# Attention on one core: both value parts in one stationary operand, and one channel summed on GpSimd

## The chip, the cores and the metric

The kernel runs on one core of one Trainium2 chip. A core has five engines that run beside each other: TensorE (PE: matmuls into PSUM), VectorE (DVE), ScalarE (ACT), GpSimd (POOL), and SyncE (SP), which here issues the DMA transfers. The metric is device time in microseconds of one execution, as the median of the runs.

## The reference

One step of a hybrid encoder layer for a prompt of 2048 rows and a sample of 32 rows with 2048 cached rows. A front stage normalises the rows and projects them. The change lies in the prompt's attention, eight heads of width 64:

```python
logits = einsum('bqhd,bkhd->bhqk', qblk, k) * scale
logits = logits + cq[..., None] - ck[:, :, None, :]     # running sums of log forget gates
logits = where(k_pos <= q_pos, logits, -inf)
probs = softmax(logits, axis=-1)
att = einsum('bhqk,bkhd->bqhd', probs, v)
...
y_b = att * silu(z_b)
```

Matrices are fp32, and the kernel splits each operand of a product into a high part that TensorE takes (fp32r) and the low rest, and adds three products: high by high, high by low, low by high.

## The kernel before, in words

**Stages.** The program is written out by hand for each engine, as one list of instructions with semaphore waits; nothing is scheduled by a planner. The front stage runs to about 1070 us of the trace, the prompt's attention (`prompt_attention`) from 1071.7 to about 1478 us, then come the sample's attention, the merge and the output norm.

**A head.** The eight heads run one after the other. A head has 40 steps: four query blocks q = 0 to 3 of 512 queries, and in block q the key blocks kb = 0 to 4q+3 of 128 keys. Steps 0 to 3 are q = 0, 4 to 11 are q = 1, 12 to 23 are q = 2, and 24 to 39 are q = 3. The last four key blocks of each q lie on the diagonal and are 512, 384, 256 and 128 columns wide; the other 24 steps of a head are 512 wide. In a step:

- TensorE makes the scores of the step three ahead (`scores`, L1668 and L1669, and a small mask matmul L1671 on the diagonal) into one of four PSUM banks, at most two row-maximum tiles for the next head (`unit`, L1701), and three value products for this step (`values`, L1685 to L1687) into one of two PSUM banks `o_bank`.
- ScalarE takes the exponential twice (`probs`, L1747 and L1748), once as the rounded high part `p_hi` and once whole.
- VectorE subtracts to get `p_lo` (`low`, L1778), reduces the row-maximum tiles (L1786, L1789; 40 in a head, in steps 0 to 29), copies a finished `o_bank` to SBUF (`take`, L1809) and, after step 9's work (`INVERT = 9`), takes the reciprocal of the last head's sums (`invert`, L1768).
- GpSimd scales, gates and splits the last head's rows (L1847, L1852, L1856), at steps set by `FINISH`.

`p_hi`, `p_lo` and the score banks are rings of four slots. The stationary operand of a value product has 64 value columns; the other 64 columns are ones in `v_hi` and zeros in `v_lo`, so that row 64 of `o_bank` is the softmax's sum.

**SyncE's list for a head h** (`sync`), in order: store the fourth sum of head h-1, load the sums as columns (L1587), store the reciprocals (L1591), load them as rows (L1595), load `zb` (L1624), the six loads of head h+1 (`load_main`, L1611 and L1613), three loads of head h+2 (`load_max`, L1605), further loads for the sample in heads 1 and 7, and then stores of sums and of the last head's rows. An issue waits for its turn in this one list. Each transfer of the six is 512 KB.

The functions that the change touches follow with the profile's line numbers.

## Time and profile before

| What | us |
|---|---|
| median of 3 runs | 1914.37 (1910.13 to 1914.48) |
| the profiled execution | 1912.48, of which span 1910.5 |
| prompt's attention in it | 1071.7 to about 1478 |
| a middle head in it (first value product to the next head's) | about 52 |

The span is the time from the first to the last instruction that the profiler saw. A group of rows below is a part of one view of that execution. A start is counted from the span's start. "idle before" is the time in which an engine waited, with what ended the wait.

### The profile page before, as it was taken

How to read it: one execution, taken by the hardware profiler on the slowest of the kernel's cores; microseconds unless marked ns; L12 is line 12 of the kernel's file. 1: busy time of each engine (PE TensorE's matmuls, PEld its weight loads, DVE VectorE, ACT ScalarE, POOL GpSimd, SP SyncE). 2: the span in 40 equal slices, each digit the busy share in tenths (PEclk: the TensorE clock that was granted, in tenths of full speed). 3: DMA queues.
4: the chain of work that ended last, by engine and by line, in shares of the span. 5: the costliest groups of instructions: out<-in, count | busy, mean ns of one | idle time of the engine just before them, and what ended most of it. 6: DMA issues, size and time to landing. Idle time of an engine off the chain costs nothing.

```text
span 1910.5 us, 28723 instructions
## 1 busy us (share of the span) xinstructions
PE 1862.7 (97%) x10604; PEld 1724.0 (90%) x10604; DVE 1295.1 (68%) x2255; ACT 854.3 (45%) x1594; POOL 185.9 (10%) x153
## 2 busy tenths in 40 slices
PE   7899999999999999999999999999999899999998
PEld 6899999999999999999999787788778799998885
DVE  8878787954545365444656588888896734457887
ACT  5545546634344443433323577777778600111100
POOL 1000000000000000000000202333333400000111
PEclk9999999999999999999999999999999999999999
DMA  6798897969889886879897816666654796765442
GB/s 225 242 329 287 314 327 278 319 233 321 269 289 315 286 297 219 298 236 326 265 303 236 211 28 121 127 134 134 134 106 142 235 377 218 246 183 160 142 144 74
DMA packets 272782, 435.99 MB, mean 228 GB/s; under 512 B 63252, under 2 KB 139188, under 8 KB 268508
## 3 DMA queue, kind: packets, MB, share of 16 engines
q1 hardware_dynamic: 266884, 425.64, 71.0%
q10 hardware_dynamic: 5760, 8.52, 1.2%
q8 instruction: 85, 1.39, 0.3%
q14 instruction: 53, 0.43, 0.1%
HBM read 285.18 MB, written 148.78 MB: 227 GB/s over the span
## 4 chain that ended last, share of the span: by engine, by line
PE 81%; DVE 7%; DMA 4%; SPq 2%; issue 2%; ACT 2%; POOL 1%; POOLq 0%; DVEq 0%; ACTq 0%
PE fr_b L639 4%; PE fr_c L639 4%; PE fr_b L640 4%; PE fr_b L641 4%; PE fr_c L640 4%; PE fr_c L641 4%; PE fr_a L640 4%; PE fr_a L639 4%; PE fr_a L641 4%; PE ln_b L2541 3%; PE ln_b L2543 3%; PE ln_b L2542 3%; PE at_o L1685 3%; PE at_m L1701 3%; PE at_s L1669 3%; PE at_s L1668 3%
## 5 line engine op out<-in xcount | busy, mean ns | idle before, releaser
L815 ACT ACTIVATE fr_wq<-fr_raw 128x512 fp32r<-128x512 f32 x288 | 178.3, 628 | 208.9 <-PE fr_d L641 137.9
L1778 DVE TENSOR_TENSOR at_p_lo<-at_s,at_p_hi 128x512 fp32r<-128x512 f32 (+1 forms) x320 | 191.9, 603 | 42.7 <-ACT at_s L1748 41.1
L1747 ACT ACTIVATE at_p_hi<-at_s 128x512 fp32r<-128x512 f32 (+1 forms) x320 | 169.8, 531 | 83.7 <-PE at_s L1669 49.1
L1105 DVE TENSOR_TENSOR fr_wq<-fr_raw,fr_wq 128x512 fp32r<-128x512 f32 x288 | 192.2, 683 | 11.4 <-ACT fr_wq L815 8.2
L639 PE MATMUL fr_b<-fr_xh,fr_wq 128*128 128x348 f32 x568 | 185.4, 326 | 7.8 <-DVE fr_wq L1105 4.0
L639 PE MATMUL fr_a<-fr_xh,fr_wq 128*128 128x348 f32 x568 | 183.9, 324 | 0.6 <-ACT fr_p L898 0.6
L639 PE MATMUL fr_c<-fr_xh,fr_wq 128*128 128x348 f32 x568 | 183.7, 323 | 0.4 <-DMA fr_wq<-w_mixed 0.4
L640 PE MATMUL fr_a<-fr_xl,fr_wq 128*128 128x348 f32 x568 | 183.4, 323 | 0.0
L641 PE MATMUL fr_b<-fr_xh,fr_wq 128*128 128x348 f32 x568 | 183.4, 323 | 0.0
L640 PE MATMUL fr_b<-fr_xl,fr_wq 128*128 128x348 f32 x568 | 183.2, 323 | 0.0
L641 PE MATMUL fr_a<-fr_xh,fr_wq 128*128 128x348 f32 x568 | 182.8, 322 | 0.0
L640 PE MATMUL fr_c<-fr_xl,fr_wq 128*128 128x348 f32 x568 | 182.4, 321 | 0.0
L641 PE MATMUL fr_c<-fr_xh,fr_wq 128*128 128x348 f32 x568 | 182.2, 321 | 0.0
L1748 ACT ACTIVATE at_s<-at_s 128x512 f32<-128x512 f32 (+1 forms) x320 | 168.7, 527 | 0.0
L1291 DVE TENSOR_TENSOR fr_res<-fr_c,fr_u 128x348 f32<-128x348 f32 x71 | 36.9, 520 | 175.8 <-PE fr_c L641 175.6
L1685 PE MATMUL at_o<-at_p_hi,at_main 128*128 128x512 f32 (+1 forms) x320 | 123.4, 386 | 0.5
L1786 DVE TENSOR_REDUCE at_piece_max<-at_m 128x1 f32<-128x512 f32 x168 | 114.3, 683 | 6.1 <-PE at_m L1701 5.9
L1669 PE MATMUL at_s<-at_qm,at_km 68*128 68x512 f32 (+1 forms) x320 | 117.8, 368 | 0.0
L1668 PE MATMUL at_s<-at_main 128*128 128x512 f32 (+1 forms) x320 | 117.6, 367 | 0.1
L975 ACT ACTIVATE fr_res<-fr_a 128x348 f32<-128x348 f32 x71 | 32.7, 461 | 189.7 <-PE fr_a L641 183.0
L1686 PE MATMUL at_o<-at_p_lo,at_main 128*128 128x512 f32 (+1 forms) x320 | 117.3, 367 | 0.0
L1687 PE MATMUL at_o<-at_p_hi,at_main 128*128 128x512 f32 (+1 forms) x320 | 117.1, 366 | 0.0
(390 smaller groups left out, 4681.3 us busy)
## 6 DMA issues: line engine op xcount, KB each, us to landing
fr_wq<-w_mixed SPq DMA_DIRECT2D x192, 512.0 KB, 5.5
fr_raw<-w_tiles SPq DMA_DIRECT2D x96, 512.0 KB, 5.2
w_mixed<-fr_wq SPq DMA_DIRECT2D x96, 512.0 KB, 4.6
mg_gates<-merge_gates SPq DMA_DIRECT2D x40, 416.0 KB, 4.8
fr_raw<-w_tiles SPq DMA_DIRECT2D x48, 256.0 KB, 5.3
merge_gates<-fr_res SPq DMA_DIRECT2D x32, 348.0 KB, 6.3
mixed<-mg_mixed ACTq DMA_DIRECT2D x40, 208.0 KB, 4.2
ln_h<-h_rows SPq DMA_DIRECT2D x16, 512.0 KB, 3.3
```

Of the source, the lines that this page charges most:

```text
L639: pe.matmul(to, wh[:, idx, k, :], xh[:, idx, k, :], start=first, stop=False, skip_group_check=skip)
L640: pe.matmul(to, wh[:, idx, k, :], xl[:, idx, k, :], start=False, stop=False, skip_group_check=skip)
L641: last = pe.matmul(to, wl[:, idx, k, :], xh[:, idx, k, :], start=False, stop=end, skip_group_check=skip)
L815: act.activation(wh[:, idx], operand(i, idx), ACT.Copy).then_inc(w_hi[idx], 1)
L1105: dve.tensor_tensor(wl[:, idx], operand(i, idx), wh[:, idx].bitcast(F32), ALU.subtract).then_inc(w_lo[idx], 1)
L1668: pe.matmul(bank[:, cols], ks[:, b, keys], qs[:, b, asked], start=True, stop=False)
L1669: last = pe.matmul(bank[:, cols], km[h % 3][:, keys], qm[h % 3][:, asked], start=False, stop=not diagonal)
L1685: pe.matmul(o, v_hi[:, b, kb, :], p_hi[:, r, cols], start=(kb == 0), stop=False)
L1686: pe.matmul(o, v_hi[:, b, kb, :], p_lo[:, r, cols], start=False, stop=False)
L1747: act.activation(p_hi[:, r, cols], s_bank[r][:, cols], ACT.Exp, scale=SCALE)
L1748: act.activation(s_bank[r][:, cols], s_bank[r][:, cols], ACT.Exp, scale=SCALE).then_inc(p_done, 1)
L1778: dve.tensor_tensor(p_lo[:, r, cols], s_bank[r][:, cols], p_hi[:, r, cols].bitcast(F32), ALU.subtract)\
```

## The change

A value product's stationary operand now holds both parts of the values: columns 0 to 63 the high part and 64 to 127 the low part (`v_both`). One product with `p_hi` and one with `p_lo` give high by high, low by high and both with `p_lo`, in rows 0 to 63 and 64 to 127 of `o_bank`. The first low channel (column 64) is overwritten with ones, so that row 64 is still the sum. What this channel would have given is made in another way: in most steps by a third product with `v_first`, which has that channel in column 0 and zeros elsewhere; in the steps for which `pooled` holds (odd kb off the diagonal: steps 5 and 7, 13, 15, 17, 19, and 25, 27, 29, 31, 33, 35) GpSimd multiplies `p_hi` with the channel and adds it up in `acc` (`first_channel`), and one more product for each of q = 1, 2, 3 brings `acc` into row 0 (`close`).

The two halves of `o_bank` are added: ScalarE copies the upper rows to `part`, one of eight buffers (`copy_part`), and `take` becomes a multiply-and-add of `part` and `o_bank` (`lanes` is one, and zero for row 64). Sums, reciprocals and their transfers go by the block q in place of once for a head, and the tables `INVERT` to `TAKE_AT` say at which step of which head (0 this one, 1 the one before) each is done. SyncE's list has another order. In the front stage the first head's low values are loaded right behind its high ones. In the diff below a line of "..." stands for lines left out.

```diff
             def load_lead_v(x, of):
-                sp.dma_start(v0[x][:, :, 0:HD].bitcast(F32), of[0:SEQ, 0:HD].rearrange("(b p) c -> p b c", p=P))\
+                at = slice(x * HD, (x + 1) * HD)
+                sp.dma_start(v0[0][:, :, at].bitcast(F32), of[0:SEQ, 0:HD].rearrange("(b p) c -> p b c", p=P))\
                   .then_inc(lead.v_in, 16)
...
         ks, qs = main[:, :, 0], main[:, :, 1]
-        v_hi, v_lo = (main[:, :, 2 + x].rearrange("p a (b c) -> p a b c", c=P) for x in range(2))
+        v_both, v_first = (main[:, :, 2 + x].rearrange("p a (b c) -> p a b c", c=P) for x in range(2))
+        first_row = sb("first_row", [P, P], 29184, F32R)
+        acc = sb("acc", [P, QW], 29312, F32R)
+        lanes = sb("lanes", [P, 1], 29824)
+        part = sb("part", [P, 2 * NQ, QW], 34880)
...
-        INVERT = 9
-        FINISH = {20 + 4 * q + x + x // 2: (q, x) for x in range(3) for q in range(NQ)}
-        FINISH_LOW = {st + 5: q for st, (q, x) in FINISH.items() if x == 0}
+        INVERT = {15: (0, 0), 23: (0, 1), 33: (0, 2), 12: (1, 3)}
+        SCALE_AT = {22: (0, 0), 37: (0, 1), 0: (1, 2), 20: (1, 3)}
+        GATE_AT = {23: (0, 0), 38: (0, 1), 1: (1, 2), 21: (1, 3)}
+        UPPER_AT = {26: (0, 0), 0: (1, 1), 4: (1, 2), 23: (1, 3)}
+        LOWER_AT = {36: (0, 0), 2: (1, 1), 8: (1, 2), 24: (1, 3)}
+        V_AT = 10
+        PART_AT = {(e + 5) % NS: (0 if e + 5 < NS else 1, q) for q, e in enumerate(ends)}
+        TAKE_AT = {(e + 4) % NS: (0 if e + 4 < NS else 1, q) for q, e in enumerate(ends)}
         TURN = 32
+
+        def pooled(st):
+            q, kb = steps[st]
+            return kb < 4 * q and kb % 2 == 1
+
...
+        def added_through(h, q):
+            return pooled_through(h, ends[q]) - 3 * h - q
+
+        def at_step(plan, h, st):
+            back, q = plan.get(st, (0, None))
+            h -= back
+            return (h, q) if q is not None and h >= 0 else None
...
+        def sums_load(sp, h, q):
+            sp.wait_ge(sum_out, 16 * (NQ * h + q) + 16)
+            sp.dma_start(sums[:, 4 * q:4 * q + 4], s["sums"][h:h + 1, q * QW:(q + 1) * QW].rearrange("a (p b) -> (a p) b", p=P))\
+              .then_inc(sums_in[q], 16)
...
+        def rcp_load(sp, h, q):
+            sp.wait_ge(rcp_out, 16 * (NQ * h + q) + 16)
+            if h:
+                sp.wait_ge(y_scaled, NQ * (h - 1) + q + 1)
+            sp.dma_start(rcp_all[:, q * QW:(q + 1) * QW], s["rcps"][h:h + 1, q * QW:(q + 1) * QW].broadcast_to([HD, QW]))\
+              .then_inc(rcp_in[q], 16)
...
             for h in range(H):
                 if h == 0:
                     sp.dma_start(mask[:, :], causal).then_inc(const_in, 16)
-                if h:
-                    sum_store(sp, h - 1, 3)
-                    sums_load(sp, h - 1)
-                    rcp_store(sp, h - 1)
-                    rcp_load(sp, h - 1)
+                if h > 1:
+                    sp.wait_ge(y_gated, NQ * (h - 1))
                 sp.dma_start(zb[:, h % 2], s["zb"][h * HD:(h + 1) * HD, 0:SEQ]).then_inc(zb_in[h % 2], 16)
                 if h + 1 < H:
                     if h:
-                        sp.wait_ge(pv_done, NS * h + RING)
+                        sp.wait_ge(closed, 3 * h)
                     load_main(h + 1)
                 if h + 2 < H:
                     if h == 0:
...
                 if h == H - 1:
                     sam.key_loads(sp)
+                if h:
+                    sum_store(sp, h - 1, 3)
+                    y_store(sp, h - 1, 1)
+                    sums_load(sp, h - 1, 3)
                 sum_store(sp, h, 0)
+                if h:
+                    y_store(sp, h - 1, 2)
+                sums_load(sp, h, 0)
+                if h:
+                    rcp_store(sp, h - 1, 3)
+                    rcp_load(sp, h - 1, 3)
+                rcp_store(sp, h, 0)
                 sum_store(sp, h, 1)
+                rcp_load(sp, h, 0)
+                sums_load(sp, h, 1)
+                rcp_store(sp, h, 1)
                 if h:
-                    y_store(sp, h - 1, 0)
...
                     max_rows(sp, h + 1)
-                if h:
-                    y_store(sp, h - 1, 2)
-                    y_store(sp, h - 1, 3)
+                rcp_load(sp, h, 2)
+                if h < H - 1:
+                    y_store(sp, h, 0)
...
                 cols = slice(d * P, QW)
                 if h == 0 and st == 0:
                     pe.wait_ge(lead.v_in, 32)
+                if st == 0:
+                    pe.wait_ge(v_ready, 2 * h + 2)
                 if kb == 0:
                     pe.wait_ge(o_read, NQ * h + q + 1)
                 pe.wait_ge(lo_done, NS * h + st + 1 + RING)
                 r = st % RING
                 o = o_bank[q % 2][:, cols]
-                pe.matmul(o, v_hi[:, b, kb, :], p_hi[:, r, cols], start=(kb == 0), stop=False)
-                pe.matmul(o, v_hi[:, b, kb, :], p_lo[:, r, cols], start=False, stop=False)
-                pe.matmul(o, v_lo[:, b, kb, :], p_hi[:, r, cols], start=False, stop=(kb == 4 * q + 3))\
-                  .then_inc(pv_done, 1)
+                pe.matmul(o, v_both[:, b, kb, :], p_hi[:, r, cols], start=(kb == 0), stop=False)
+                last = pe.matmul(o, v_both[:, b, kb, :], p_lo[:, r, cols], start=False, stop=False)
+                if not pooled(st):
+                    last = pe.matmul(o, v_first[:, b, kb, :], p_hi[:, r, cols], start=False, stop=(q == 0 and kb == 3))
+                last.then_inc(pv_done, 1)
+
+            def close(h, q):
+                if h == 0 and q == 1:
+                    pe.wait_ge(first_row_set, 2)
+                pe.wait_ge(acc_done, added_through(h, q))
+                pe.matmul(o_bank[q % 2][:, :], first_row[:, :], acc[:, :], start=False, stop=True).then_inc(closed, 1)
 
...
                     values(h, b, st)
+                    if h and st == 0:
+                        close(h - 1, NQ - 1)
+                    if st - 1 in ends[1:-1]:
+                        close(h, ends.index(st - 1))
...
+                before = (h, st - RING) if st >= RING else (h - 1, st - RING + NS)
+                if before[0] >= 0 and pooled(before[1]):
+                    act.wait_ge(acc_scaled, pooled_through(*before))
                 act.activation(p_hi[:, r, cols], s_bank[r][:, cols], ACT.Exp, scale=SCALE)
                 act.activation(s_bank[r][:, cols], s_bank[r][:, cols], ACT.Exp, scale=SCALE).then_inc(p_done, 1)
+
+            def copy_part(h, q):
+                n = NQ * h + q
...
+                    act.wait_ge(o_read, n - 2 * NQ + 3)
...
             def take(h, b, q):
-                dve.wait_ge(pv_done, NS * h + ends[q] + 1 + RING)
+                dve.wait_ge(part_done, NQ * h + q + 1)
                 if h > 1:
                     dve.wait_ge(yl_done, NQ * (h - 1))
-                dve.tensor_copy(y[:, b, q * QW:(q + 1) * QW], o_bank[q % 2][0:HD + 1, :]).then_inc(o_read, 1)
+                o = o_bank[q % 2]
+                dve.scalar_tensor_tensor(out=y[0:HD, b, q * QW:(q + 1) * QW], in0=part[HD:2 * HD, (NQ * h + q) % (2 * NQ), :], scalar=lanes[HD:2 * HD, :],
+                                         in1=o[0:HD, :], op0=ALU.mult, op1=ALU.add).then_inc(o_read, 1)
...
+            def free_first_channel(h):
+                b = h % 2
+                if h:
+                    pool.wait_ge(main_in[b], used(h, 2, 96))
+                else:
+                    pool.wait_ge(lead.v_in, 32)
+                pool.tensor_copy(v_first[:, b, :, 0:1], v_both[:, b, :, HD:HD + 1].bitcast(F32)).then_inc(v_ready, 1)
+                pool.wait_ge(v_ready, 2 * h + 1)
+                pool.memset(v_both[:, b, :, HD:HD + 1].bitcast(F32), 1.0).then_inc(v_ready, 1)
...
-            for h in range(1, H):
+            def first_channel(h, st):
+                q, kb = steps[st]
+                r, n = st % RING, pooled_through(h, st)
+                own = v_first[:, h % 2, kb, 0:1].bitcast(F32)
+                pool.wait_ge(p_done, NS * h + st + 1)
+                if kb == 1:
+                    if n > 1:
+                        pool.wait_ge(closed, 3 * h + q - 1)
+                    pool.tensor_scalar(acc[:, :], p_hi[:, r, :].bitcast(F32), own, None, ALU.mult).then_inc(acc_scaled, 1)
+                else:
+                    added = n - 3 * h - q
+                    if added > 1:
+                        pool.wait_ge(acc_done, added - 1)
+                    pool.tensor_scalar(term[:, :], p_hi[:, r, :].bitcast(F32), own, None, ALU.mult).then_inc(acc_scaled, 1)
+                    pool.wait_ge(acc_scaled, n)
+                    pool.tensor_tensor(acc[:, :], acc[:, :].bitcast(F32), term[:, :], ALU.add).then_inc(acc_done, 1)
+
+            for h in range(H):
                 for st in range(NS):
-                    if st in FINISH_LOW:
-                        lower(pool, h - 1, 1 - h % 2, FINISH_LOW[st])
-                    if st in FINISH and FINISH[st][1] < 2:
-                        (scale, gate)[FINISH[st][1]](pool, h - 1, 1 - h % 2, FINISH[st][0])
+                    if h + 1 < H and st == V_AT:
+                        free_first_channel(h + 1)
```

SyncE's list at a middle head before, from the loads of the next head on: `sums` is the store of a block's sums, `at_sums` the load of sums that the reciprocal reads, `yb_hi` and `yb_lo` the stores of finished rows.

```order
L1591 DMA rcps<-at_rcp 128x16
L1595 DMA at_rcp_all<-rcps 64x2048
L1624 DMA at_zb<-silu_zb 64x2048
L1611 DMA at_main<-k_hi 64x2048
L1611 DMA at_main<-q_lo 64x2048
L1611 DMA at_main<-k_lo 64x2048
L1611 DMA at_main<-q_hi 64x2048
L1613 DMA at_main<-v_hi 128x16x64
L1613 DMA at_main<-v_lo 128x16x64
L1605 DMA at_km_50<-k_hi 64x2048
L1605 DMA at_qm_52<-q_hi 64x2048
L1605 DMA at_km_50<-forget_rows 2x2048
```

The same place of the change, from the second of the six loads on:

```order
L1636 DMA at_main<-q_lo 64x2048
L1636 DMA at_main<-k_lo 64x2048
L1636 DMA at_main<-q_hi 64x2048
L1638 DMA at_main<-v_hi 128x16x64
L1638 DMA at_main<-v_lo 128x16x64
L1630 DMA at_km_50<-k_hi 64x2048
L1630 DMA at_qm_52<-q_hi 64x2048
L1630 DMA at_km_50<-forget_rows 2x2048
L1602 DMA sums<-at_part 1x512
L1597 DMA yb_hi<-at_y_hi 64x512
L1597 DMA yb_lo<-at_y_lo 64x512
L1607 DMA at_sums<-sums 128x4
```

Before, the reciprocals of the last head were stored and loaded ahead of the nine loads; now the store of that head's fourth block of sums, two row stores and the load `at_sums` for the fourth reciprocal stand behind them.

VectorE's list before, around the reciprocal (`RECIPROCAL`), in a middle head; a 128x256 subtraction is that of step 10, so this is the end of step 9's work:

```order
L1778 TENSOR_TENSOR at_p_lo<-at_s,at_p_hi 128x256
L1786 TENSOR_REDUCE at_piece_max<-at_m 128x1
L1768 RECIPROCAL at_rcp<-at_sums 128x16
L1778 TENSOR_TENSOR at_p_lo<-at_s,at_p_hi 128x128
L1786 TENSOR_REDUCE at_piece_max<-at_m 128x1
L1778 TENSOR_TENSOR at_p_lo<-at_s,at_p_hi 128x512
```

The change's reciprocals of the last head's fourth block and of this head's first block:

```order
L1855 TENSOR_REDUCE at_piece_max<-at_m 128x1
L1837 RECIPROCAL at_rcp<-at_sums 128x4
L1847 TENSOR_TENSOR at_p_lo<-at_s,at_p_hi 128x512
L1858 ISA at_m,at_piece_max<-at_m,at_wide_mask 128x256
L1858 ISA at_piece_max 128x1
L1847 TENSOR_TENSOR at_p_lo<-at_s,at_p_hi 128x512
L1855 TENSOR_REDUCE at_piece_max<-at_m 128x1 x2
L1847 TENSOR_TENSOR at_p_lo<-at_s,at_p_hi 128x512
L1858 ISA at_m,at_piece_max<-at_m,at_wide_mask 128x384
L1858 ISA at_piece_max 128x1
L1879 SCALAR_TENSOR_TENSOR at_y<-at_part,at_lanes,at_o 64x512
L1837 RECIPROCAL at_rcp<-at_sums 128x4
```

The reciprocal that needs the last block of the head before has moved from the end of step 9's work to the end of step 12's, behind three more subtractions and four more reductions.

## Rows read from the trace of the kernel before

**Rows 1.** The page, busy time, share of the span and instructions of engines.

```profile
PE 1862.7 (97%) x10604; PEld 1724.0 (90%) x10604; DVE 1295.1 (68%) x2255; ACT 854.3 (45%) x1594; POOL 185.9 (10%) x153
```

**Rows 2.** Windows: start:end, us, busy of PE, PEld, DVE, ACT, POOL, clock, DMA share, GB/s.

```profile
1276.00:1328.00 52.00, 51.86 (x259) 41.62 (x259) 46.50 (x104) 39.77 (x86) 15.32 (x13) 1.00 0.60 123
...
1435.00:1478.00 43.00, 43.00 (x226) 35.59 (x225) 27.03 (x46) 37.64 (x84) 15.24 (x12) 1.00 0.51 151
```

**Rows 3.** Windows inside the middle head, about steps 0-11, 12-30, 31-39.

```profile
1281.00:1296.20 15.20, 15.15 (x80) 12.46 (x79) 14.38 (x40) 10.83 (x25) 0.00 (x0) 1.00 0.02 2
1296.20:1322.00 25.80, 25.80 (x121) 20.53 (x120) 25.19 (x53) 20.04 (x40) 12.62 (x10) 1.00 1.04 204
1322.00:1332.90 10.90, 10.81 (x62) 8.56 (x60) 7.08 (x16) 8.82 (x22) 2.63 (x3) 1.00 0.37 102
```

**Rows 4.** Timeline of TensorE, same head: start us, duration us.

```profile
1280.97 0.44 PE L1685 MATMUL at_o<-at_p_hi,at_main 128*128 128x512 f32 x1
...
1287.33 0.40 PE L1685 MATMUL at_o<-at_p_hi,at_main 128*128 128x512 f32 x1
...
1287.80 0.39 PE L1687 MATMUL at_o<-at_p_hi,at_main 128*128 128x512 f32 x1
```

**Rows 5.** Timeline of VectorE, same head, from the reciprocal to step 12's last reduction.

```profile
1293.95 0.24 DVE L1768 RECIPROCAL at_rcp<-at_sums 128x16 f32<-128x16 f32 x1
...
1297.18 0.68 DVE L1786 TENSOR_REDUCE at_piece_max<-at_m 128x1 f32<-128x512 f32 x1
```

**Rows 6.** Timeline of SyncE's DMA issues, same head: start us, duration us of an issue.

```profile
1295.65 0.48 SPq L1595 DMA_DIRECT2D at_rcp_all<-rcps  x1
1296.17 0.60 SPq L1624 DMA_DIRECT2D at_zb<-silu_zb  x1
1296.82 0.60 SPq L1611 DMA_DIRECT2D at_main<-k_hi  x1
...
1300.18 12.62 SPq L1613 DMA_DIRECT2D at_main<-v_lo  x1
1317.50 0.54 SPq L1582 DMA_DIRECT2D sums<-at_y  x2
```

**Rows 7.** DMA issues of that head: KB each, median us from issue to landing.

```profile
at_main<-v_lo SPq DMA_DIRECT2D x1, 512.0 KB, 20.4
```

**Rows 8.** The same, of 1317.3 to 1319.2 us alone.

```profile
yb_hi<-at_y_hi SPq DMA_DIRECT2D x1, 128.0 KB, 5.4
```

**Rows 9.** The tile yb_hi: landing of all its stores.

```profile
DMA to landing us min/median/max: 2.2/2.4/12.1
```

**Rows 10.** The tile at_sums: landing of all its loads.

```profile
DMA to landing us min/median/max: 1.5/1.6/4.3
```

**Rows 11.** SyncE's waits, six heads: us in total, times, longest.

```profile
SPq L1587 <- DMA sums<-at_y: 5.4, 6, 0.9
```

**Rows 12.** SyncE's issues in head 1: the sample's early loads, first issue and the issue behind.

```profile
1160.14 2.04 SPq L1969 DMA_DIRECT2D sa_q_hi<-q_hi  x2
...
1167.92 0.35 SPq L1582 DMA_DIRECT2D sums<-at_y  x1
```

**Rows 13.** SyncE's issues in head 7: first key load and the issue behind them.

```profile
1448.02 4.85 SPq L1981 DMA_DIRECT2D sa_k_rows<-cache_k  x4
...
1457.27 0.56 SPq L1582 DMA_DIRECT2D sums<-at_y  x2
```

**Rows 14.** Windows around the start of attention: columns as in rows 3.

```profile
1064.00:1067.40 3.40, 0.00 (x0) 0.01 (x1) 0.52 (x1) 0.49 (x1) 0.02 (x1) 1.00 1.19 238
...
1071.60:1075.00 3.40, 3.40 (x10) 2.92 (x11) 1.25 (x6) 1.04 (x4) 2.61 (x4) 0.50 1.11 273
```

**Rows 15.** Groups by form, GpSimd: count, busy us, mean ns, idle before.

```profile
L1847 POOL TENSOR_TENSOR at_y<-at_y,at_rcp_all 64x512 f32<-64x512 f32 x32 | 42.0, 1317 | 213.7 <-DMA at_rcp_all<-rcps 213.7
...
L1865 POOL MEMSET at_main<- 128x1024 f32 x1 | 1.0, 957 | 0.1
```

**Rows 16.** Groups by form, VectorE: the copy of o_bank.

```profile
L1809 DVE COPY at_y<-at_o 65x512 f32<-65x512 f32 x32 | 21.8, 681 | 1.9 <-PE at_o L1687 1.9
```

More of the change, by code:

```diff
@@ L1760, in scalar, with invert @@
                         copy_rows(h + 1)
[L1761 to L1765 removed]
+                    if at_step(PART_AT, h, st):
+                        copy_part(*at_step(PART_AT, h, st))
+                    job = at_step(UPPER_AT, h, st)
+                    if job and job[0] < H - 1:
+                        upper(act, job[0], job[0] % 2, job[1])
+            copy_part(H - 1, NQ - 1)
+        def invert(dve, h, q):
+            dve.wait_ge(sums_in[q], 16 * h + 16)
             if h:
[L1767 to L1768 removed]
+                dve.wait_ge(rcp_out, 16 * (NQ * (h - 1) + q) + 16)
+            dve.reciprocal(rcp[:, 4 * q:4 * q + 4], sums[:, 4 * q:4 * q + 4]).then_inc(rcp_done, 1)
         st_.invert = invert
@@ L1869, in gpsimd @@
             sam.clear_queries(pool)
-            for h in range(1, H):
-                for st in range(NS):
-                    if st in FINISH_LOW:
-                        lower(pool, h - 1, 1 - h % 2, FINISH_LOW[st])
-                    if st in FINISH and FINISH[st][1] < 2:
-                        (scale, gate)[FINISH[st][1]](pool, h - 1, 1 - h % 2, FINISH[st][0])
+            def first_channel(h, st):
[7 more added lines that the diff above has]
+                    pool.tensor_scalar(acc[:, :], p_hi[:, r, :].bitcast(F32), own, None, ALU.mult).then_inc(acc_scaled, 1)
+                else:
+                    added = n - 3 * h - q
[5 more added lines that the diff above has]
+            for h in range(H):
+                for st in range(NS):
+                    if h + 1 < H and st == V_AT:
+                        free_first_channel(h + 1)
+                    if pooled(st):
+                        first_channel(h, st)
+                    for plan, what in ((LOWER_AT, lower), (SCALE_AT, scale), (GATE_AT, gate)):
+                        job = at_step(plan, h, st)
+                        if job and job[0] < H - 1:
+                            what(pool, job[0], job[0] % 2, job[1])
         st_.sync, st_.tensor, st_.scalar, st_.vector, st_.gpsimd = sync, tensor, scalar, vector, gpsimd
```

103 lines of the change are left out of this document (52 added, 51 removed).

## The prediction

> **What bounds the kernel now.** I read the page first: TensorE is busy for 97% of the span, VectorE for 68% and GpSimd for 10% [rows 1]. That speaks for taking products from TensorE and giving work to GpSimd. But the 97% is a mean over stages, so I next read windows of the stage that is changed. In a middle head of 52.0 us TensorE is busy 51.86 and VectorE 46.50; in the last head, which has no row-maximum tiles to reduce, VectorE has only 27.03 of 43.0 [rows 2]. Cut into three, the middle head shows two bounds: VectorE is busy 14.38 of 15.2 us in the first third and 25.19 of 25.8 in the second, and only 7.08 of 10.9 in the last, where ScalarE has 8.82 [rows 3]. So a product taken from TensorE shows in full only where VectorE has room, about steps 31 to 39. Last I read who feeds VectorE: its reciprocal waits for a load that SyncE issues from one list, so SyncE's issues and their landings are part of the path as soon as that load is late.
>
> **What is saved.** Two products of 512 columns start 0.47 us after each other (1287.33 to 1287.80), so one costs 0.235 us [rows 4]. The change takes 12 of them from a head and adds 3 closing ones: 9 x 8 x 0.235 = 16.9 us of TensorE's time in all. Of this, steps 5 and 7 lie in the first third and seven of the twelve in the second. There VectorE, whose work doesn't shrink, has 0.8 and 0.6 us left, so I count 0.5 us for both. In the last third three products fall away, 0.7 us. VectorE gains three small reciprocals a head; the present one takes 0.24 us and the next instruction followed it within that time [rows 5], so 0.5 us more. That leaves 0.7 us for each of seven heads, and 2 us for the last, where only ScalarE, at 37.64 of 43.0, is near: together 7 us. The bounds are 16.9 (VectorE never in the way) and 2 (only the last head). The multiply-and-add that takes the place of the copy is not in the trace; the copy takes 681 ns [rows 16], and I take the same, with the reading of a second operand from SBUF as the doubt that the lower bound covers. ScalarE's four copies a head lie in its free 12 us [rows 2].
>
> **GpSimd.** A head gets 12 multiplications and 9 additions of 128x512. The nearest rows are a two-input operation of 64x512 at 1317 ns and a memset of 128x1024 at 957 ns, so 0.48 for 512 columns [rows 15]: an addition is taken at 1.32, a multiplication lies between 0.48 and 1.32. With 12 scale, gate and split operations of 1.32 the head's sum is 33 to 44 us of 52, so it has room on average and costs nothing where nothing else is late; if it were the bound, ScalarE would wait for it, since a slot of `p_hi` is refilled four steps later. The Trainium skill, GPSIMD Engine Reference, section 3.1, gives 769 ns for a one-input loop over 512 elements: by that a multiplication would be 0.77 us and the sum would stay as it is.
>
> **What becomes late.** This is the large term. `at_sums` of the last head's fourth block now stands in SyncE's list behind the nine loads for later heads, and VectorE waits for it at the end of step 12's work. I set both on one clock, from the head's first value product at 1280.97 [rows 4].
>
> VectorE's side: step 12's last reduction starts at 1297.18, and the one-after-another pace is 0.6 us (subtraction and reduction overlap a little), so VectorE asks at about 1297.8, which is +16.8 [rows 5].
>
> SyncE's side: the loads may start when the head before is closed, after the first products, at about +1.2 (three products and a closing one, 0.94 us, and the semaphore). In the trace 20.7 us pass between the issue of the first of the six loads and that of the sums behind the nine (1296.82 to 1317.50), above all because the issue of `v_lo` is held for 12.62 us [rows 6]. There, two transfers of 512 KB, `rcp_all` and `zb`, had been issued within 1.2 us ahead of them. The window moves 204 GB/s [rows 3], so one such transfer takes 2.6 us, and without both the distance would be 15.5. In the change `zb` and a row store still go ahead but some 2 us earlier; I take 17. The sums are then issued at +18.2. A store that was issued at that place landed after 5.4 us [rows 8], where such stores take 2.4 in the median and 12.1 at most [rows 9]; so it lay 3 us behind what was in the queue. The sums alone land within about 1.1 (0.22 for the issue and a wait of at most 0.9 [rows 11]); behind the loads 4.2, at +22.4. `at_sums` then needs 0.35 for its issue and 1.6 us to land [rows 10]: +24.4. VectorE waits 24.4 - 16.8 = 7.6 us. TensorE has about 1.2 us of work in hand meanwhile (five products, 5 x 0.235), so 6.4 us are lost. At the low end (distance 15.5, landing 1.1, load 1.5) the sums are there at +19.7 and 1.7 are lost; at the high end (20.7, 5.4, 4.3) at +32, and 14 are lost. Behind the waiting reciprocal stand all of VectorE's subtractions, so every engine waits, and VectorE has no room in the second third to win it back.
>
> By head: heads 2 to 5 lose 4 x 6.4 = 25.6. In head 1 the sample's early loads stand in the same list, 7.8 us of issues (1160.14 to 1167.92) [rows 12], while the queue drains: issue at +26, landing 2, load 2, so +30, less 16.8 and 1.2: 12. In head 6 three of the nine loads are missing, 4.7 us of issues (1312.80 to 1317.50) [rows 6]; the queue is then longer, 5 us to land: +20.4, 2.4 lost. In head 7 the key loads take 9.25 us of issues [rows 13]; 1 + 9.25 + 5 + 2 = +17.2 against VectorE's asking at about +13, since its steps take five products, 1.2 us: 3 lost. Head 0 asks only for its own first block, after step 15, and its loads start ahead of the head: 0.5, at most 3. Sum 43.5 us (low end 16, of which head 1 has 9.5; high end about 90).
>
> **The clock.** Before attention TensorE is idle for the 3.40 us from 1064.0; a few us later its granted clock is 0.50, which is 1.2 GHz, from 1071.6 to 1075.0, with 10 products in 3.4 us [rows 14]. Stalls of 6 us in heads 1 to 5 may do the same. At half the clock at most half of such a stretch's work is lost, 1.7 us; I take 1.6 for each of five heads, 8 us (0 to 22, if all seven stalls cost two such stretches).
>
> **The sum.** 43.5 + 8 - 7 = +44.5 on the profiled execution's 1912.48: 1957. That execution lies 0.1% below the median of the runs, which changes nothing here.
>
> **The rivals.** (A) Faster: the sums come in time. This needs them by +16.8 and so 7.6 us earlier than I have them; then only the saving is left, 1912.5 - 7 = 1905 (1896 if it shows in full). For it speaks that the queue is clear when the loads start earlier; against it, that even the low end is late by 2.9 us. The Trainium skill, DMA: Bandwidth & Descriptors, section Bandwidth, has 341 GB/s for a load of 1 MB; by that the nine loads would be through in about three fifths of the time, and the sums just in time. The trace has 204 GB/s in that very window, and I go by the trace. (B) No change: the sums come in time, but GpSimd's wait for the next head's values at step 10 (`V_AT`) takes the place. `v_lo` landed 23.8 us after the first load's issue (1300.18 + 20.4 - 1296.82) [rows 6, 7]; less 3.7 as above, that is +21.3. After two small operations and a multiplication, at +23, ScalarE may refill step 17's slot, about 2 us after it would; six heads lose 2 each, 1912.5 + 12 - 7 = 1918. In my forecast this wait lies inside VectorE's longer one. (C) Slower still: GpSimd at its upper price and blocked from about +9 to +21 needs 44 + 12 = 56 us of a head that lasts 52 + 7; it decides only from 59 us on, and would then add 2 to 4 us a head, some 20: 1977.
>
> **How the numbers follow.** My forecast has 0.76, A 0.10, B 0.07, C 0.07. The time is the forecast's, 1957. The range runs from 1912, where the low end of the waits meets the full saving (1912.5 + 16 + 0 - 16.9), to 2000, past C and most of the way to the high end (1912.5 + 90 + 22 - 2 = 2022, which needs every bound at once). It leaves out A and the last tail, some 15 in 100. A change under 0.3% (5.7 us) can't be told from none here: faster 0.10 (A), same 0.07 (B), slower 0.83.
>
> **What would show it.** Right: VectorE's reciprocal waits for `at_sums` seven times, 2 to 13 us each, longest in head 1; SyncE's issue of `v_lo` still takes over 10 us; heads 1 to 5 last 57 to 64 us; after some stalls the granted clock falls. Wrong: `at_sums` lands before VectorE asks, heads under 52 us; or the longest wait in a head is ScalarE's for GpSimd; or subtractions, 0.68 us now, get longer beside GpSimd's new work.

## The result and the profile after

The changed kernel takes 1998.98 us (1997.66 to 2003.53, 4 runs) against 1912.43 (1910.13 to 1914.48, 4 runs) of the kernel before: a ratio of 1.0463, with an interval of 1.0446 to 1.048. The forecast was +44.5 us; it is +86.5. The profiled execution has a span of 2001.7 us. Its page, engines and the granted clock in 40 slices, beside [rows 1]:

```profile
PE 1895.4 (95%) x10532; PEld 1736.4 (87%) x10532; DVE 1307.8 (65%) x2281; ACT 872.6 (44%) x1626; POOL 428.1 (21%) x337
PEclk8999999999999999999998988898989999999999
```

The clock row of the kernel before:

```profile
PEclk9999999999999999999999999999999999999999
```

TensorE is busy longer with 72 matmuls fewer, and from the 22nd to the 30th slice, which is attention, the clock row has 8s. All of the loss lies there. From the first to the last value product attention took 405.4 us before and takes 499.2; from then to the end it is 433.4 and 433.5. The table cuts each head by the starts of its first value products (us, summed over eight heads; the granted clock's record gives the last column):

| | steps 0-11 | 12-23 | 24-30 | 31-39 | sum | at half clock |
|---|---|---|---|---|---|---|
| before | 123.8 | 128.6 | 77.3 | 75.7 | 405.4 | 3.3 |
| after | 174.0 | 170.9 | 80.3 | 73.9 | 499.2 | 104.3 |

A middle head (head 4) lasts 65.4 us instead of 51.9. Windows of its steps 0 to 11, 12 to 30 and 31 to 39, as [rows 3]:

```profile
1325.70:1347.30 21.60, 17.67 (x83) 13.97 (x81) 15.44 (x40) 14.64 (x33) 11.94 (x10) 0.92 1.00 198
1347.30:1381.80 34.50, 28.43 (x119) 21.87 (x118) 26.43 (x57) 21.39 (x42) 24.96 (x20) 0.90 0.28 57
1381.80:1391.10 9.30, 9.08 (x53) 6.92 (x53) 6.04 (x12) 6.04 (x16) 8.71 (x7) 1.00 0.05 16
```

No engine is busy throughout in the first two any more: everyone waits. In the last third, where VectorE had room, 0.4 us is gained (the windows here and in [rows 3] are cut at slightly different places; by the starts of the value products, steps 31 to 39 of head 4 took 9.8 and take 9.4). Three waits of the view of waits, over all of attention (us in total, times, longest), show on whom:

```profile
POOL at_main L1941 <- DMA at_main<-v_lo: 47.7, 7, 9.4
ACT at_y_hi L1782 <- POOL at_y L1925: 36.5, 14, 3.7
DVE at_rcp L1837 <- DMA at_sums<-sums: 28.2, 7, 7.3
```

The third is the wait that was forecast: seven times, six of them behind step 12 and one in head 0, for its own first block. The second was not: ScalarE, in order, waits at the split of the last head's rows for GpSimd's gate. The chain of waits that ends with the sums that VectorE needs in head 4, in order of time:

```profile
1331.25 10.54 SPq L1638
...
1341.83 3.27 SPq L1630
...
1345.78 0.46 SPq L1630
1346.24 0.04 issue
1346.29 6.57 DMA sums<-at_part
1352.86 0.02 issue
1352.88 1.58 DMA at_sums<-sums
1354.46 0.02 issue
1354.48 0.18 DVE at_rcp L1837
...
1356.48 0.43 PE at_o L1724
```

The issue of `v_lo` is held for 10.54 us, the sums' 2 KB need 6.57 us behind the loads, and VectorE starts its reciprocal at +28.8 from the head's first value product (1325.7). In the last row it is 0.43 us from the start of a value product of 512 columns to the next; at the full clock it was 0.235 [rows 4]. Windows around that wait show why (the clock is the third number from the end):

```profile
1344.60:1348.00 3.40, 3.40 (x20) 2.78 (x19) 3.31 (x9) 2.88 (x6) 0.00 (x0) 1.00 1.11 222
1348.00:1351.40 3.40, 2.13 (x10) 1.44 (x8) 0.47 (x1) 2.45 (x5) 2.42 (x4) 1.00 0.92 201
1351.40:1354.80 3.40, 0.00 (x0) 0.00 (x0) 0.32 (x2) 0.67 (x2) 3.15 (x3) 0.92 0.18 53
1354.80:1358.20 3.40, 2.51 (x6) 2.03 (x7) 3.17 (x7) 0.00 (x0) 1.97 (x2) 0.50 0.35 72
1358.20:1361.60 3.40, 3.40 (x10) 2.74 (x10) 2.56 (x6) 2.01 (x4) 0.00 (x0) 0.58 0.15 39
1361.60:1365.00 3.40, 3.40 (x19) 2.53 (x19) 3.11 (x7) 2.12 (x5) 3.05 (x3) 1.00 0.29 42
```

TensorE has nothing at all in the third row, and from 1354.3 its clock is at 0.50, which is 1.2 GHz, for 6.8 us: 10 products in 3.4 us, and 19 when it is back. Attention has 14 such stretches of 3.4 to 13.7 us; one of them, at its start, was there before [rows 14]. The Trainium skill, TensorE: Matmul & The Clock Gate, section "HAM oscillation — how this bites in real kernels", tells of a kernel in which a wait for a load in every tile makes every tile start at the low clock; the trace agrees, with one or two stretches in each head.

GpSimd's groups by form (count, busy us, mean ns):

```profile
L1969 POOL TENSOR_SCALAR at_term<-at_p_hi,at_main 128x512 f32<-128x512 f32 x72 | 112.5, 1563 | 39.2 <-ACT at_s L1802 31.7 <-POOL at_acc L1971 7.5
L1971 POOL TENSOR_TENSOR at_acc<-at_acc,at_term 128x512 fp32r<-128x512 f32 x72 | 92.4, 1283 | 6.0
L1964 POOL TENSOR_SCALAR at_acc<-at_p_hi,at_main 128x512 fp32r<-128x512 f32 x24 | 37.5, 1564 | 49.0 <-ACT at_s L1802 31.1 <-PE at_o L1734 17.9
```

A multiplication takes 1.56 us, above the upper bound of 1.32. The six pooled steps of the fourth block lie in steps 24 to 35, which last 15.5 us, so GpSimd runs late at the end of each head. Its timeline, and ScalarE's, where head 4 ends:

```profile
1386.97 1.56 POOL L1969 TENSOR_SCALAR at_term<-at_p_hi,at_main 128x512 f32<-128x512 f32 x1 [0.17 <-POOL at_acc L1971]
1388.62 1.29 POOL L1971 TENSOR_TENSOR at_acc<-at_acc,at_term 128x512 fp32r<-128x512 f32 x1
1389.87 1.28 POOL L1929 TENSOR_TENSOR at_y_lo<-at_y,at_y_hi 64x512 fp32r<-64x512 f32 x1
1391.11 1.28 POOL L1920 TENSOR_TENSOR at_y<-at_y,at_rcp_all 64x512 f32<-64x512 f32 x1
1392.47 1.26 POOL L1925 TENSOR_TENSOR at_y<-at_y,at_zb 64x512 f32<-64x512 f32 x1
```

```profile
1389.50 0.60 ACT L1802 ACTIVATE at_s<-at_s 128x512 f32<-128x512 f32 x1
1393.76 0.63 ACT L1782 ACTIVATE at_y_hi<-at_y 64x512 fp32r<-64x512 f32 x1 [3.66 <-POOL at_y L1925]
```

Multiplications and additions alternate from 1373.0 to 1389.9 with no gap over 0.2 us. Then come a split, a scale and a gate, and only after the gate may ScalarE go on: 3.66 us without an exponential, and a stretch of 13.7 us at half clock behind it.

### The profile page after: what moved, and what is told of

Read it like the earlier page. It is cut to its first block and busy times, and to the rows that moved or that the text cites. A ratio compares the mean times of both kernels' runs of the same rounds, so it can differ in the third digit from the quotient of the medians.

```text
span 2001.7 us, 29064 instructions
## 1 busy us (share of the span) xinstructions
PE 1895.4 (95%) x10532; PEld 1736.4 (87%) x10532; DVE 1307.8 (65%) x2281; ACT 872.6 (44%) x1626; POOL 428.1 (21%) x337
## 5 line engine op out<-in xcount | busy, mean ns | idle before, releaser
L1801 ACT ACTIVATE at_p_hi<-at_s 128x512 fp32r<-128x512 f32 (+1 forms) x320 | 168.9, 528 | 122.8 <-PE at_s L1706 73.9
L1724 PE MATMUL at_o<-at_p_hi,at_main 128*128 128x512 f32 (+1 forms) x320 | 134.3, 420 | 28.5 <-DVE at_p_lo L1847 27.8
L1412 POOL TENSOR_TENSOR fr_small<-fr_small 128x1 f32<-128x1 f32 (+1 forms) x18 | 12.3, 686 | 615.3 <-DVE fr_small L1075 615.3
L1747 PE MATMUL at_m<-at_km,at_qm 66*128 66x512 f32 (+2 forms) x280 | 113.0, 431 | 31.6 <-DVE at_piece_max L1858 21.0
L1705 PE MATMUL at_s<-at_main 128*128 128x512 f32 (+1 forms) x320 | 127.0, 397 | 0.0
L1706 PE MATMUL at_s<-at_qm,at_km 68*128 68x512 f32 (+1 forms) x320 | 126.0, 394 | 0.0
L1725 PE MATMUL at_o<-at_p_lo,at_main 128*128 128x512 f32 (+1 forms) x320 | 125.8, 393 | 0.0
```

The source lines that it names most:

```text
L1705: pe.matmul(bank[:, cols], ks[:, b, keys], qs[:, b, asked], start=True, stop=False)
L1706: last = pe.matmul(bank[:, cols], km[h % 3][:, keys], qm[h % 3][:, asked], start=False, stop=not diagonal)
L1724: pe.matmul(o, v_both[:, b, kb, :], p_hi[:, r, cols], start=(kb == 0), stop=False)
L1725: last = pe.matmul(o, v_both[:, b, kb, :], p_lo[:, r, cols], start=False, stop=False)
L1801: act.activation(p_hi[:, r, cols], s_bank[r][:, cols], ACT.Exp, scale=SCALE)
```

## The experiments

All are edits of the changed kernel but the last three. Lengths of a head's parts are those of heads 2 to 6 unless said otherwise. A time without a ratio is that of a single execution. In the edits, `...` stands for code left out, and only the telling lines are shown.

**Are the late sums and GpSimd's products the cause? (inv_late, no_pool, both.)** The first moves VectorE's reciprocals and what hangs on them later, the second takes GpSimd's products away (a third product in every step, and the closing products add zeros), the third does both.

```diff
-        INVERT = {15: (0, 0), 23: (0, 1), 33: (0, 2), 12: (1, 3)}
+        INVERT = {20: (0, 0), 26: (0, 1), 33: (0, 2), 19: (1, 3)}
```

```diff
-            return kb < 4 * q and kb % 2 == 1
+            return False
```

> The reciprocal of the last head's fourth block moves from step 12 to step 19 (and those of this head's first two blocks to 20 and 26, with scale, gate, upper and lower behind them), so VectorE no longer asks before the sums have landed. Theory 1, two stalls a head: the wait at step 12 with the low clock after it makes up the growth of steps 12 to 23 (42 us over eight heads), and GpSimd's lateness that of steps 0 to 11 (51 us). Then steps 12 to 23 fall from 18 to 25 us a head to about 17, steps 0 to 11 stay at 22 to 25, time 1955 to 1970. Theory 2, GpSimd alone: VectorE's wait lies in the shadow of GpSimd's lateness, and the time stays above 1985.

> GpSimd sums no channel: every step takes the third product, and the closing products add zeros, so the result is whole. Theory 1: steps 0 to 11 go back to about 16 us a head (from 22 to 25), but VectorE then asks for the sums some 5 us sooner after the head's start, so the wait at step 12 grows to 7 to 9 us and steps 12 to 23 to 25 us or more: time 1960 to 1985. Theory 2, GpSimd alone: both thirds go back, time 1915 to 1930.

> No channel on GpSimd and the late reciprocal together. Theory 1: both stalls are gone, no low clock inside the heads; what is left is three closing products a head, four ScalarE copies and the smaller sums: 1912 to 1925. If a third cost is hidden in the rest of the change (the copies, the quarter sums, the other order of the loads), it shows here as more than 1930.

Measured: 2005.19, 1982.53 and 1959.73 us (ratio of the third 1.0259, 1.024 to 1.0279). Only the step-12 wait did what I thought: with late reciprocals steps 12 to 23 are back at 16.9 to 17.2 us, from up to 25. The time is not, for each wait moved on. The view of waits, of the first, the second and the third kernel:

```profile
ACT at_y_hi L1782 <- POOL at_y L1925: 51.7, 15, 3.9
```

```profile
DVE at_rcp L1836 <- DMA at_sums<-sums: 45.4, 9, 9.8
```

```profile
ACT at_y_hi L1781 <- POOL at_y L1924: 28.3, 7, 4.8
```

In the first, ScalarE's wait grew from 36.5 to 51.7 us; in the second, VectorE is no longer held up at step 0, asks sooner and waits 45.4 us (42.9 without the last of the nine, which is behind attention) instead of 28.2; in the third the reciprocals come so late that ScalarE waits for the gate at step 25. So theory 1 in its simple form, that the two waits seen are the whole loss and go when they are taken away, fell: the third kernel should have taken 1912 to 1925 us. Theory 2, GpSimd alone, fell too, since no_pool stays at 1982.53.

**Does step 0's wait go if ScalarE asks later? (upper_late.)**

```diff
-        UPPER_AT = {26: (0, 0), 0: (1, 1), 4: (1, 2), 23: (1, 3)}
+        UPPER_AT = {26: (0, 0), 4: (1, 1), 7: (1, 2), 23: (1, 3)}
```

> ScalarE's copy of the second block's finished rows moves from step 0 to step 4 of the next head (the third block's from 4 to 7, GpSimd's splits behind them), GpSimd's work unchanged. Theory 1a, the wait of ScalarE at step 0 is what makes GpSimd's lateness cost: steps 0 to 11 fall by 4 to 6 us a head, and part of it comes back in the wait at step 12; time 1965 to 1985. Theory 1b, GpSimd's backlog itself bounds the head's start (through the ring of four slots): steps 0 to 11 stay above 21 us, time above 1990.

Measured: 1995.84 us. Steps 0 to 11 fall from 22-25 to 17.3 us, as theory 1a has it, but steps 12 to 23 rise to 28.2-30.9 in heads 1 to 5, so the time is that of 1b:

```profile
DVE at_rcp L1837 <- DMA at_sums<-sums: 64.3, 8, 12.5
ACT at_y_hi L1782 <- POOL at_y L1925: 7.8, 7, 1.7
```

28.7 us less on ScalarE, 36.1 more on VectorE: the two waits stand in one row, and either hides part of the other.

**Is it GpSimd's price or its places? (mult_tt, all_late, all_late_tt.)** The multiplication is written with two inputs, the factor repeated along the row; all deadlines are moved late; both.

```diff
-pool.tensor_scalar(term[:, :], p_hi[:, r, :].bitcast(F32), own, None, ALU.mult).then_inc(acc_scaled, 1)
+pool.tensor_tensor(term[:, :], p_hi[:, r, :].bitcast(F32), own.broadcast_to([P, QW]), ALU.mult).then_inc(acc_scaled, 1)
```

```diff
-        UPPER_AT = {26: (0, 0), 0: (1, 1), 4: (1, 2), 23: (1, 3)}
+        UPPER_AT = {37: (0, 0), 13: (1, 1), 17: (1, 2), 34: (1, 3)}
...
-        V_AT = 10
+        V_AT = 21
```

> The change with one edit: GpSimd multiplies by a two-input operation with the channel repeated along the row, in place of the operation with one scalar a partition that took 1.56 us. Theory 1 with the price as cause of the head's late start: 1.28 us each, so the chain of six in steps 25 to 35 ends 1.7 us sooner, ScalarE's wait at step 0 falls from 3.7 to about 2, steps 0 to 11 to 18 to 21 us; part of it comes back at step 12, time 1975 to 1995. If this operation is no cheaper: 1999.

> The change with GpSimd's full work, but each deadline moved to where its result should be there: reciprocals at 19, 20, 26 and 33, scale and gate at 24 to 30 and at the next head's 0 to 3, ScalarE's copies at 13, 17, 34 and 37, values at 21, row stores behind the sums in SyncE's list. Theory 1, deadlines alone: heads of 52 to 54 us, 1913 to 1930. Theory 3, GpSimd's capacity: 12 multiplications of 1.56, 9 additions of 1.28 and 12 other operations of 1.28 are 46 us of a head of 52, and with waits between them some deadline is still missed: 1945 or more.

> As the run with all deadlines late, with the two-input multiplication. Theory 1: within 5 us of that run, at 1912 to 1925. Theory 3: lower than it by 10 us or more, since GpSimd gets 3.4 us a head back.

Measured: 1979.1, 1953.07 (ratio 1.0225, 1.021 to 1.0241) and 1931.58 us. The group of mult_tt, beside 1563 ns above:

```profile
L1969 POOL TENSOR_TENSOR at_term<-at_p_hi,at_main 128x512 f32<-128x512 f32 x72 | 75.0, 1042 | 61.7 <-ACT at_s L1802 57.6 <-POOL at_acc L1971 0.4
```

With this alone steps 0 to 11 come down to 18.3 us, near the 17.3 of the later place in upper_late: GpSimd's price and ScalarE's place made that wait together, and either takes it away. Steps 12 to 23 are at 24 to 25 us in heads 2 to 5. With late deadlines alone steps 0 to 23 are 17.3 and 16.9, but steps 31 to 39 rise from 9.4 to 13.3, and the view of waits of all_late names GpSimd's multiplication, which holds the ring of `p_hi`:

```profile
ACT at_p_hi L1800 <- POOL at_term L1968: 39.6, 34, 2.1
```

The shorter multiplication takes 21.5 us off this version, and with it ScalarE waits for GpSimd's multiplications only in head 7, 2 us in all; theory 3 holds in both runs. So GpSimd is a bound at the end of a head, not on its average.

**What do the copies and closing products cost? (old_recip, copy_early, late_tt_half, old_copy_early, all.)** old_recip has no products on GpSimd and takes sums, reciprocals and loads once for a head in the old order. copy_early (from all_late_tt) and old_copy_early (from old_recip) take the bank one step sooner, `PART_AT` like `TAKE_AT`; late_tt_half (from all_late_tt) has half of the pooled steps; `all` joins copy_early and late_tt_half.

```diff
-        TAKE_AT = {(e + 4) % NS: (0 if e + 4 < NS else 1, q) for q, e in enumerate(ends)}
+        TAKE_AT = {(e + 3) % NS: (0 if e + 3 < NS else 1, q) for q, e in enumerate(ends)}
```

> One part of the change undone: sums and reciprocals go once for a head as before, ahead of the loads, VectorE asks at step 9, GpSimd prepares the next values at step 38; no channel on GpSimd. Both value parts in one operand, the copies and closing products stay. Theory 1, deadlines: each result that comes late by the change's tables (sums for VectorE, gated rows for ScalarE) stops TensorE, and when one is moved the wait turns up at the next; with none late the heads last 52 to 54 us, time 1913 to 1930. Theory 2, a fixed cost: the new operand, copies or closing products cost it by themselves, and time stays above 1940.

> The version with all deadlines late and the two-input multiplication (1931.6 us, a middle head 54.7 us: 17.2 in steps 0 to 11, 16.9, 10.1, 10.5), with ScalarE's copy of the upper rows and VectorE's multiply-and-add that takes the bank one step earlier each. In the version before it TensorE waits 1.1 us in steps 0 to 11 of a head for that multiply-and-add, which frees the bank of the head's second block. Theory bank: the accumulator bank comes free too late, since two engines now read it one after the other; then steps 0 to 11 fall from 17.2 to about 16.2 us and the time to 1922 to 1926. Rival theory copy: what costs is the work itself, 4 copies on ScalarE and the longer operation on VectorE; then steps 0 to 11 stay at 17 or more and the time at 1929 to 1934.

> The version with all deadlines late and the two-input multiplication, with six instead of twelve pooled steps in a head, so six third products go back to TensorE (1.4 us a head) and GpSimd has about 14 us less. If GpSimd's capacity is what makes steps 31 to 39 last 10.5 us and head 7's steps 24 to 30 9.2 us, they fall to 9.3 and 8.3, and the time from 1931.6 to about 1923. If TensorE's work bounds these steps, they get longer by up to 0.7 us and the time is 1931 to 1940.

> The version without GpSimd's products and with the whole-head sums and loads in their order of before (1928.7 us, a middle head 54.6 us: 17.2, 17.2, 10.4, 9.8), with the same two operations one step earlier. Theory bank: steps 0 to 11 fall by about 1 us a head and the time to 1919 to 1923. Theory copy: 1926 to 1931.

> All together: deadlines late, two-input multiplication, half of the pooled steps, copy and multiply-and-add one step earlier. If the theories of the capacity and of the bank both hold, the gains add: 1931.6 less 8 less 7, so 1914 to 1919, level with before (1911). If only one holds 1922 to 1926; if the saving on TensorE showed in full as well it would be under 1908.

Measured: 1928.67 (ratio 1.0092, 1.0075 to 1.0109), 1931.44 (1.0106, 1.0092 to 1.0119), 1929.88, 1926.63 (1.0078, 1.0064 to 1.0091) and 1928.42 (1.008, 1.0065 to 1.0094). Taking the bank sooner left steps 0 to 11 at 17.2 us: that theory fell. Half of the pooled steps bring steps 31 to 39 from 10.5 to 10.0, a third of what I expected. The run `all`, at 1928.42, lies above what its theories gave. In the traces of old_recip and late_tt_half head 0 is some 4 us longer than in the others, with 17.1 us at half clock at the start of attention, so their times are not to be compared to a few us. Some 15 us stay, without late sums and without GpSimd's products.

**Where are these 15 us? (no_copy, no_close, layout_only.)** Edits of old_copy_early (1926.6 us): without ScalarE's copies (VectorE's multiply-and-add, 744 ns, goes with them and the copy of before, 679 ns, comes back), without closing products, without both.

```diff
-                dve.scalar_tensor_tensor(out=y[0:HD, ...], in0=part[...], scalar=lanes[...], in1=o[0:HD, :], op0=ALU.mult, op1=ALU.add).then_inc(o_read, 1)
+                dve.tensor_copy(y[:, b, q * QW:(q + 1) * QW], o[0:HD + 1, :]).then_inc(o_read, 1)
```

> The version without GpSimd's products and with the old order of sums and loads (1926.6 us; a middle head 54.6 us: 17.2, 17.1, 10.5, 9.8), without ScalarE's four copies a head: VectorE copies the lower 64 rows and the row of sums out of the bank in one operation, as the kernel before does. The upper rows, the low parts of the values for 63 of 64 channels, are left out of the output. Theory copy (the extra reading of each bank, 0.63 us on ScalarE with VectorE behind it, costs what is left): steps 0 to 11 fall to 15.7 to 16.0, 12 to 23 to 16.5 to 16.8, the time to 1911 to 1916. Rival theory close (the closing product, which a bank has to wait for): 17.0 or more, 1923 to 1927.

> The same version with the copies, but without the 23 closing products (they add zeros here): a block ends with its last third product. Theory close: steps 0 to 11 fall to 15.7 to 16.0 and the time to 1911 to 1917. Theory copy: 17.0 or more in steps 0 to 11; only the products' own 3 x 0.235 us a head may come off, so 1921 to 1927.

> Both left out, the copies (with the upper rows' share of the output) and the closing products: what remains of the change is the layout of the values, GpSimd's two small operations a head and the one-step-later place of VectorE's copy. If nothing of these costs anything, the time is that of before, 1909 to 1916, a middle head 51.9 us; above 1918 something third has a price.

Measured: 1918.15 (1.0039, 1.0026 to 1.0051), 1922.92 (1.0058, 1.0038 to 1.0078) and 1912.49 (1.0013, 1.0003 to 1.0023). Both have a part, and they add up: head 4 lasts 52.6 us without both, 53.3 with closing products, 53.9 with copies, 54.6 with both, so 0.7 and 1.3 us a head. Without both, 0.7 us stay above the 51.9 of before, as the price of the layout with what goes with it. Windows of its steps 0 to 11, of layout_only and of old_copy_early:

```profile
1282.30:1298.60 16.30, 15.81 (x83) 12.87 (x82) 14.80 (x41) 11.19 (x25) 0.00 (x0) 1.00 0.02 2
```

```profile
1287.30:1304.60 17.30, 16.14 (x84) 13.10 (x84) 15.42 (x41) 12.32 (x28) 0.00 (x0) 1.00 0.02 2
```

ScalarE is busy 1.1 us more here and VectorE 0.6, and the stretch is 1.0 longer, though ScalarE is busy for only 71% of it. Of the 1.3 us a head VectorE's longer operation is 4 x 0.065, so 0.3; whether the rest is ScalarE's work or the order in which the two engines read the bank is not separated.

**What does the half clock cost by itself? (stall3, stall6, stall9.)** Edits of the kernel before: a stall of known length on VectorE in heads 1 to 7.

```diff
+            if h < H - 1:
+                for i in range(3):
+                    dve.tensor_reduce(rcp[:, i:i + 1], wide_mask[:, :], AX_X, ALU.max).then_inc(late, 1)
+                dve.wait_ge(late, 3 * (h + 1))
             dve.reciprocal(rcp[:, :], sums[:, :]).then_inc(rcp_done, 1)
```

> The kernel before, with a stall of known length: in heads 1 to 7 VectorE makes three needless reductions of 128x512 ahead of its reciprocal, behind step 9. At 0.6 us one after another they take 1.9 us, of which VectorE's slack and TensorE's work in hand cover about 1. Theory plain (a stall costs its own length): 7 x 0.9, so +4 to +9 us on 1911. Theory clock (each longer idle of TensorE is followed by a stretch at half clock): no different here, since TensorE is idle for less than 1 us a head.

> Six needless reductions, 3.7 us in each of seven heads. Theory plain: 7 x 2.7, so +17 to +22. Theory clock: the same, and 1.7 us or more on top in each head in which the granted clock falls; at all seven +29 to +45.

> Nine needless reductions, 5.5 us in each of seven heads. Theory plain: 7 x 4.5, so +29 to +35. Theory clock: 1.7 to 5 us more a head, from one to three half-clock stretches of 3.4 us like those in the trace of the changed kernel: +43 to +66, with 24 to 72 us at half clock in the heads.

Measured: 1929.4 (1.0099, 1.0083 to 1.0116), 1945.82 (1.0186, 1.017 to 1.0201) and 1962.7 (1.0267, 1.0247 to 1.0287): +18, +35 and +52 us. The last two are as the clock theory has it. At the shortest stall both theories had +4 to +9 and both missed: the clock fell there already, and even without it the stall cost 1.6 us a head, not 0.9. In stall3 the stall itself is one row of VectorE's timeline in head 4:

```profile
1297.87 1.86 DVE L1770 TENSOR_REDUCE at_rcp<-at_wide_mask 128x1 f32<-128x512 f32 x3
```

In each of heads 1 to 6 TensorE then idles once for the same 1.47 us; here in heads 3 and 4, each with a window behind it:

```profile
1247.30 0.50 PE L1701 MATMUL at_m<-at_km,at_qm 66*128 66x512 f32 x1 [1.47 <-DVE at_piece_max L1790]
1300.82 0.50 PE L1701 MATMUL at_m<-at_km,at_qm 66*128 66x512 f32 x1 [1.47 <-DVE at_piece_max L1790]
```

```profile
1248.80:1252.20 3.40, 3.40 (x17) 2.79 (x16) 3.40 (x8) 2.90 (x6) 0.00 (x0) 1.00 0.95 214
1301.90:1305.30 3.40, 3.40 (x10) 2.62 (x10) 2.34 (x5) 1.56 (x3) 0.00 (x0) 0.50 0.81 178
```

The same idle was followed by half clock in heads 2, 4, 5 and 6 and not in heads 1 and 3; why is not shown. So the heads price the clock: head 3, in which it stayed at 1.00, lasts 53.5 us, 1.6 above before; heads 2, 4 and 5, with one stretch of 3.4 us at half clock, 55.0 to 55.1; head 6, with 6.8 us, 56.5. In stall9 the stall of head 4 is 5.42 us:

```profile
1318.71 5.42 DVE L1770 TENSOR_REDUCE at_rcp<-at_wide_mask 128x1 f32<-128x512 f32 x9
```

By head 3 of stall3 that alone would cost some 5.1 us (an estimate). Heads 3 and 5, with 6.8 us at half clock, lie 7.2 above before, head 2, with as much, 8.0, and heads 4 and 6, with 10.2 us, 8.2. So 3.4 us at half clock cost 1.0 to 1.5 us here. Windows of head 4 in stall9, from within the stall on:

```profile
1320.80:1324.20 3.40, 0.00 (x0) 0.00 (x0) 3.37 (x7) 0.44 (x1) 0.00 (x0) 0.65 0.00 0
1324.20:1327.60 3.40, 2.39 (x7) 2.10 (x8) 3.10 (x8) 0.07 (x1) 0.00 (x0) 0.50 0.19 41
1327.60:1331.00 3.40, 3.40 (x10) 2.63 (x10) 1.98 (x5) 1.93 (x4) 0.31 (x1) 0.50 1.04 229
```

No version beats the kernel before; of those that compute everything, old_copy_early is nearest.

## Why the prediction was wrong

The sign, the step-12 wait and its cause were right; the size was half of what came, because GpSimd's work was put at nothing and the clock at a quarter. The parts of the 93.8 us that attention lost, worked out: old_copy_early's attention is 423.7 us, so copies, closing products and layout are 18; 101 us more at half clock, at 1.0 to 1.5 us for 3.4, are 30 to 44; the remaining 32 to 46 are the waits themselves. By place the loss can be read without a price for the clock: steps 0 to 11 take 174.0 us, and 134.5 without GpSimd's products (no_pool); steps 12 to 23 take 170.9, and 131.6 with late reciprocals (inv_late). So some 39 us hang on each of the two waits, half clock included, though in those two kernels waits at other places took the time back.

- **The sums at step 12: right, and near in size.** Forecast were 43.5 us of lost time, measured are 28.2 us of VectorE's waiting in the changed kernel and 42.9 in no_pool, where nothing holds VectorE up before. In head 4 the loads start at +1.9 (forecast +1.2), the sums are issued 18.7 us later (17), land in 6.57 (4.2), and `at_sums` needs 1.58 (1.6). VectorE asked 6 us later than I had it, because of a wait I did not have. By place: heads 1, 4 and 2 wait longest (7.3, 6.0 and 5.8 us), and head 6 doesn't wait.
- **GpSimd "has room on average and costs nothing where nothing else is late": this step failed.** ScalarE's wait for GpSimd's gate at step 0, 3.7 us in each of seven heads, has no term in the sum. A price was mis-sized, 1.56 us for a multiplication that I bounded at 1.32 by a two-input operation; and the sum over a head was the wrong test. Half of the work falls on steps 24 to 35, where 6 multiplications and 5 additions take 16.9 us, more than the 15.5 that these steps last. The Trainium skill, GPSIMD Engine Reference, section 3.1, which I weighed, has 769 ns for a loop with one input; this form took twice that. Steps 0 to 11 lost 50 us, some 39 of them by GpSimd (no_pool), and steps 12 to 23, with the wait that I had forecast, 42. I had named the sign ("the longest wait in a head is ScalarE's for GpSimd"), but under C I tied the price to 59 us of work a head.
- **The clock: right in kind, a quarter in size.** I took 1.6 us a head for five heads, 8 in all, and 22 as the bound. A stretch of 3.4 us costs 1.0 to 1.5, near the estimate, but the 101 us are 30 times as much, because most heads have two waits and one wait brings up to four times 3.4 us.
- **The saving of 7 us: the sign was wrong.** In the last third 0.4 us a head are gained in heads 2 to 6 (73.9 against 75.7 us in all, since head 7 loses; forecast 0.7 a head). But "ScalarE's four copies a head lie in its free 12 us" did not hold: no_copy shows 1.3 us a head for the copies and VectorE's operation behind them (744 ns, where I had taken the copy's 681), and the closing products, which I had netted against the products saved, cost 0.7. copy_early, with the products saved and no long wait left, is still 19 us slower than before. That ScalarE's idle time is not free because it stands between two others' steps is a reading that no run isolates.
- **Subtractions did not get longer** beside GpSimd's work: those of 512 columns have 0.68 us in the timeline as before. Rivals A and B fell: the sums did come late, and GpSimd's wait for `v_lo`, 47.7 us, did not take their place. In head 4 it ends at 1348.9, while VectorE waits until 1354.5; in inv_late, where it stays at step 10 with 40.4 us in all, steps 12 to 23 take 16.9 us.

How the waits and the clock share the 76 us or so that are left in the changed kernel itself stays an estimate, since the price of the clock was measured in another kernel.

## What to carry to other kernels

Cost offloaded work by the stretch where it falls, not by the engine's average, and measure the very form of the operation before counting on it. When waits stand in one row, removing one shows the next: list all deadlines behind it before pricing the removal. A stall of 1.86 us on the engine that feeds TensorE cost 1.6 us in a head in which the clock stayed and 3.1 to 4.6 where it fell.

## What the runs showed of the hardware that was not expected

- On GpSimd a multiplication of 128x512 by one factor a row took 1563 ns as a one-input operation with a scalar and 1042 ns as a two-input operation with the factor repeated; an addition of two full inputs took 1283.
- A stall of 1.86 us on VectorE, ahead of TensorE, left TensorE idle for 1.47 us in each of six heads; in four of them a stretch of 3.4 to 6.8 us at half clock followed.
- A 2 KB store behind 4.5 MB of loads landed after 6.57 us.
